# A two-block network on one Trainium2 core: the MLP's second projections in two phases, seven products for token tiles 0 and 2, residuals by halves of a tile's columns

## The reference

```python
def _sqrelu_mlp(h, w1, w2):
    return jnp.square(jax.nn.relu(h @ w1)) @ w2          # w1: 1024 x 4096, w2: 4096 x 1024
...
        x = _layer_norm(DN_ALPHA * x + (1.0 + g_t) * y, ln_g[i, 0], ln_b[i, 0])
        h = x * (1.0 + sc_c) + sh_c
        y = _sqrelu_mlp(h, mlp_w1[i], mlp_w2[i])
        x = _layer_norm(DN_ALPHA * x + (1.0 + g_c) * y, ln_g[i, 1], ln_b[i, 1])
```

## Time and profile before

| | us |
|---|---|
| median of three runs (3334.27, 3338.92, 3338.95) | 3338.92 |
| the profiled execution | 3333.77 |
| its span | 3331.80 |
| TensorE busy in it | 3149.7 |
| VectorE busy in it | 1541.2 |
| mean clock granted to TensorE, of full speed | 0.973 |
| layer 0: second projection, first to last product | 2356.9 to 2579.4 |
| layer 1: second projection, first to last product | 3098.5 to 3318.4 |

### The profile page before, as it was taken

The page is one execution under the profiler, slowest core; times in us unless marked ns, Lnnn a source line. Parts: engine busy times, 40 slices in busy tenths (PEclk is TensorE's granted clock), DMA queues, the critical chain, the costliest instruction groups (busy, mean ns, idle before and its releaser), DMA issues. The chain is left out here.

```text
span 3331.8 us, 37758 instructions
## 1 busy us (share of the span) xinstructions
PE 3149.7 (95%) x12154; PEld 1717.4 (52%) x12155; DVE 1541.2 (46%) x3359; ACT 563.3 (17%) x1281; POOL 243.0 (7%) x377
## 2 busy tenths in 40 slices
PE   7999999999998897979997988999999998999998
PEld 3445666644447332323333535488544565588543
DVE  6447676565556342334444386565103333565003
ACT  1002222200011121212222216200000233100000
POOL 1000000011100121212212000000000000000000
PEclk9999999999997998989999999999999999999999
DMA  7563133397733898997978311122221223022220
GB/s 242 167 205 96 61 98 89 102 308 241 243 127 128 327 353 336 365 358 302 349 283 288 112 56 39 51 95 76 84 104 27 79 74 133 26 95 101 76 76 25
DMA packets 261211, 532.85 MB, mean 160 GB/s; under 512 B 26249, under 2 KB 162052, under 8 KB 236522
## 3 DMA queue, kind: packets, MB, share of 16 engines
q1 hardware_dynamic: 204240, 380.16, 32.4%
q0 software_dynamic: 46992, 140.37, 12.2%
q10 hardware_dynamic: 9866, 10.82, 0.9%
HBM read 520.60 MB, written 36.83 MB: 167 GB/s over the span
## 5 line engine op out<-in xcount | busy, mean ns | idle before, releaser
L1328 PE MATMUL ps<-WR,hT 128*64 x832 | 384.8, 617 | 58.9 <-DVEq L2865 31.8
L1329 PE MATMUL ps<-WR,hT 128*64 128x512 f32 x832 | 384.8, 617 | 0.0
L1730 PE MATMUL ps<-WR 128*128 128x512 f32 x768 | 329.9, 592 | 0.0
L1328 PEld LDWEIGHTS ps<-WR,hT 128*64 128x64 f32 x832 | 117.3, 143 | 311.6 <-issue 311.6
L1730 PEld LDWEIGHTS ps<-WR 128*128 128x128 f32 x768 | 145.9, 190 | 182.8 <-issue 182.2
L2862 DVE COPY WR<-WR 128x1024 f32 x208 | 131.1, 693 | 227.1 <-SPq L646 174.0
L2625 DVE TENSOR_TENSOR WR<-ps,grow 128x1024 f32<-128x1024 f32 x20 | 24.5, 1224 | 436.3 <-PE ps L1741 368.5
L1024 PE MATMUL ps<-hT,WR 128*128 128x512 f32 x512 | 223.9, 593 | 0.6 <-DVE WR L2438 0.6
L1691 PE MATMUL ps<-WR 128*128 128x256 f32 x960 | 217.0, 379 | 0.0
L1691 PEld LDWEIGHTS ps<-WR 128*128 128x128 f32 x960 | 182.4, 190 | 24.8
L1349 PE MATMUL ps<-WR 128*64 x416 | 189.5, 598 | 3.2 <-DVEq L2875 2.1
(11 more groups left out here) (411 smaller groups left out, 4537.4 us busy)
## 6 DMA issues: line engine op xcount, KB each, us to landing
WR<-in_w_gate SPq DMA_DIRECT2D x64, 1024.0 KB, 8.7
WR<-in_w_up SPq DMA_DIRECT2D x64, 1024.0 KB, 11.3
WR<-in_w_down SPq DMA_DIRECT2D x64, 1024.0 KB, 9.1
WR<-in_mlp_w SPq DMA_DIRECT2D x32, 2048.0 KB, 7.7
xr<-in_ada_w POOLq DMA_DIRECT2D x32, 1024.0 KB, 5.6
WR<-in_w_in SPq DMA_DIRECT2D x56, 512.0 KB, 6.8
xr<-in_w_ada POOLq DMA_DIRECT2D x16, 1024.0 KB, 5.5
WR<-in_w_in SPq DMA_DIRECT2D x16, 1024.0 KB, 6.6
```

The costliest lines, as they stand in the source:

```text
L1328: mm(out[0:HALF], xT[u][:, k, 0:HALF], wa[:, :, k, :], start=(k == 0), stop=(k == KD - 1))
L1329: last = mm(out[HALF:P], xT[u][:, k, HALF:P], wb[:, :, k, :], start=(k == 0), stop=(k == KD - 1))
L1730: last = mm(ps[:, 2 * t + n, :], h1T[:, k, t * P:(t + 1) * P], w[:, k - 4 * u, 512 * n:512 * n + 512], start=(k == 0), stop=False)
```

## The change

The down stage becomes two phases. In phase 1 (`down_pair`, weights in the new stage `seven`) the outputs of token tiles 0 and 2 are made by seven products for each pair of k-tiles (k, k + 16): the blocks are the two k-tiles, the two token tiles and the two halves of 512 output columns. The row sums (`row_sums`, of h1T, 256 columns for two k at once) and the weight sums (`down_weight_sums`, 512 columns) are made by VectorE; each product has one bank and accumulates over the 16 pairs. At the end ScalarE copies p1 and VectorE adds the products into the corners `down_c` (`down_corners`, seven additions). In phase 2 the whole of w2 is loaded again, and token tiles 1 and 3 are made as before, tile 1 in banks 6 and 7, tile 3 in 4 and 5. The slots of the down stage's units are now 2, 1, 3, 2, 1, 3, 2, 1, those of `seven` are 1, 3, 2, 1, 3, 2, 1, 3; slot 0 holds sums and corners until the residual of tile 2 has read them.

The tiles of residuals 3 and 5 go in the order 0, 2, 1, 3. In layer 0 the transposes of tiles 0 and 2 stand behind units 1 and 2 of phase 2, those of tile 1 after the tenth product of tile 3, those of tile 3 at the end. `res_b` is raised once for each half of 512 columns, and every residual from banks (`by_halves`: n = 0, 2, 4 in all tiles, 3 and 5 in tiles 1 and 3) works on each half when it is there. The slots of the last weights of an output projection are given free by VectorE (`release`). In residual 5 normalizing, gain and store go by halves as well.

The diff, cut to its core. The stages `("seven0", 1, [(1, 2), (3, 2), (2, 2), (1, 2), (3, 2), (2, 2), (1, 2), (3, 2)])` and `seven1` stand ahead of the down stages.

```diff
+DOWN_BANKS = dict(p6=4, p5=0, p7=1, p4=2, p3=3, p1=6, p2=5)
+TILES_OF = {n: (0, 2, 1, 3) if n in (3, 5) else (0, 1, 2, 3) for n in range(6)}
+RES_B = {0: 0, 2: TT, 3: 2 * TT, 4: 2 * TT + 2, 5: 3 * TT + 2}
+TURN_BANK = {n: (0, 6, 2, 4) if n == 4 else (0, 2, 4, 6) for n in range(6)}
...
+        if i + 1 == UP_PAIRS:
+            v += ["t_0"] + [f"{n}_{i}" for n in CORNERS[:5]] + ["s_0"] + [f"{n}_{i}" for n in CORNERS[5:] + ("sq",)]
+        else:
+            v += [f"{n}_{i}" for n in CORNERS + ("sq",)]
+    p += [f"kp_{k}" for k in range(16)] + ["p1_end"]
+    a.append("p1_end")
+    v.append("t_1")
+    for j in range(1, 8):
+        v += [f"s_{j}", f"t_{2 * j}", f"t_{2 * j + 1}"]
+    v += [f"{n}_end" for n in CORNERS]
...
-    ("down0", 1, [(1, 1), (3, 1), (2, 1), (0, 1), (3, 1), (2, 1), (1, 1), (0, 1)]),
+    ("seven0", 1, [(1, 2), (3, 2), (2, 2), (1, 2), (3, 2), (2, 2), (1, 2), (3, 2)]),
+    ("down0", 1, [(2, 1), (1, 1), (3, 1), (2, 1), (1, 1), (3, 1), (2, 1), (1, 1)]),
...
+        down_t = [[view(WR, 512 * n, 512) for n in range(4)], [view(R, 16384 + 512 * n, 512) for n in range(4)]]
+        down_s = [[view(R, 18432 + 1024 * i + 256 * n, 2, P) for n in range(4)] for i in range(2)]
+        down_c = [view(WR, 2048 + D * i, D) for i in range(2)]
+
+        def weights_of(layer, k):
+
+            w = unit(f"seven{layer}", k // 2, 0, 4, D)
+            return [[w[:, 2 * i + k % 2, 512 * n:512 * n + 512] for n in range(2)] for i in range(2)]
...
+                    fill(f"seven{layer}", u, 0, *[(unit(f"seven{layer}", u, 2 * D * i, 2, D),
+                                                   mlp_w2[layer][:, 16 * i + 2 * u:16 * i + 2 * u + 2, :])
+                                                  for i in range(2)])
...
-            for t in range(TT):
-                sp.wait_ge(sem("res_x"), 5 * TT + t + 1)
-                sp.dma_start(out_v[:, t, :], xr[:, t, :]).then_inc(sem("out_done"), 16)
-            sp.wait_ge(sem("out_done"), 16 * TT)
+            for n, t in enumerate(TILES_OF[5]):
+                for h in range(2):
+                    sp.wait_ge(sem("res_x"), 5 * TT + 2 * n + h + 1)
+                    sp.dma_start(halves(out_v[:, t, :])[h], halves(xr[:, t, :])[h]).then_inc(sem("out_done"), 16)
+            sp.wait_ge(sem("out_done"), 2 * 16 * TT)
...
-                    if t == TT - 1 and n == KD - 1:
-                        spent(last, name, 0)
-                if hi == 2 * KD:
-                    last.then_inc(sem("res_b"), 1)
+                    if k == KD - 1:
+                        last.then_inc(sem("res_b"), 1)
...
+            def down_pair(layer, k):
+
+                name = f"seven{layer}"
+                (b11, b12), (b21, b22) = weights_of(layer, k)
+                s1, s2, s3, s4 = [v[:, k % 2, :] for v in down_s[(k // 2) % 2]]
+                t1, t2, t3, t4 = down_t[k % 2]
+                a11, a12, a22 = [h1T[:, i, t * P:(t + 1) * P] for i, t in ((k, 0), (k + 16, 0), (k + 16, 2))]
+
+                def product(p, rows, weights):
+                    if k == 0:
+                        pe.wait_ge(*bank_read(layer, DOWN_BANKS[p], 7 * (UP_PAIRS - 1)))
+                    return mm(ps[:, DOWN_BANKS[p], :], rows, weights, start=(k == 0), stop=(k == 15))
+
+                if k % 2 == 0:
+                    have(name, k // 2)
+                    pe.wait_ge(*up_v(layer, f"s_{k // 2}"))
+                pe.wait_ge(*up_v(layer, f"t_{k}"))
+                product("p6", s2, t2)
+                product("p5", s1, t1)
+                product("p7", s3, t3)
+                if k == 14:
+                    pe.wait_ge(*up_v(layer, f"sq_{UP_PAIRS - 1}"))
+                product("p4", a22, t4)
+                product("p3", s4, b22).then_inc(sem("up_p"), 1)
+                last = product("p1", a11, b11)
+                if k == 15:
+                    last.then_inc(sem("up_p"), 1)
+                last = product("p2", a12, b21)
+                if k % 2:
+                    spent(last, name, k // 2)
...
+                for k in range(16):
+                    down_pair(layer, k)
+                bank_free = {(1, 1): up_v(layer, f"c21_{UP_PAIRS - 1}"), (1, 0): up_a(layer, "p1_end"),
+                             (3, 0): up_v(layer, "u2_end"), (3, 1): up_v(layer, "c11_end")}
+                bank = {1: 6, 3: 4}
...
-                        pe.wait_ge(*up_v(layer, f"sq_{k // 2}" if k > 1 else f"sq{k}"))
-                        for t in range(TT):
-                            for n in range(2):
+                        for t in (1, 3):
+                            for n in ((1, 0) if t == 1 else (0, 1)):
                                 if k == 0:
-                                    pe.wait_ge(*bank_read(layer, 2 * t + n, 7 * (UP_PAIRS - 1)))
-                                last = mm(ps[:, 2 * t + n, :], h1T[:, k, t * P:(t + 1) * P],
+                                    pe.wait_ge(*bank_free[t, n])
+                                last = mm(ps[:, bank[t] + n, :], h1T[:, k, t * P:(t + 1) * P],
                                           w[:, k - 4 * u, 512 * n:512 * n + 512], start=(k == 0), stop=False)
                     spent(last, name, u)
+                    if layer == 0 and u in (1, 2):
+                        turn_in(2 * u - 2, xr, "res_norm", TT * 3, 4)
...
+                down_tile(1, 0, 16)
+                down_tile(3, 0, 10)
                 if layer == 0:
-                    last_turn(3, early)
+                    turn_in(1, xr, "res_norm", TT * 3, 4)
+                down_tile(3, 10, 16)
+                if layer == 0:
+                    turn_in(3, xr, "res_norm", TT * 3, 4)
...
+                for v in halves(xr[:, t, :], 2 if n == 5 else 1):
+                    A(v, v, ACT.Identity, scale=rstd[:, t:t + 1], bias=rtmp[:, 1, t:t + 1]).then_inc(
+                        sem("res_norm"), 1)
...
+                act.wait_ge(*up_p(layer, "p1_end"))
+                A(down_c[0][:, 0:512], ps[:, DOWN_BANKS["p1"], :], ACT.Copy).then_inc(sem("up_a"), 1)
...
+                def by_halves(n, t, alpha, scratch, at, done):
+
+                    for h in range(2):
+                        dve.wait_ge(sem("res_b"), done + h + 1)
+                        if t == TT - 1:
+                            release(n, h)
+                        x, g, v = [halves(w)[h] for w in (xr[:, t, :], grow[:, :], scratch)]
+                        link(V.tensor_tensor(v, ps[:, at + h, :], g, ALU.mult))
+                        link(V.scalar_tensor_tensor(x, x, alpha, v, ALU.mult, ALU.add))
+                        link.mark(V.bn_stats(stats[:, t, 6 * h:6 * h + 6], x))
+                    rms_of(t)
+                    shift_of(t)
+
+                def release(n, h):
+
+                    name, u = last_weights[n]
+                    if h == 1 or u == 1:
+                        dve.sem_inc(used[ring.slot(name, u if h else 0)], 1)
+
+                def shift_of(t):
+
+                    link(V.scalar_tensor_tensor(rtmp[:, 1, t:t + 1], mv[:, t, 0:1], -1.0, rstd[:, t:t + 1],
+                                                ALU.mult, ALU.mult))
+                    dve.sem_inc(sem("res_stats"), 1)
...
+                        at, tiles = 2 * t, TILES_OF[n]
+                        if n in (3, 5):
+                            at = {1: 6, 3: 4}.get(t)
+                            tiles = (1, 3)
+                        if t in tiles:
+                            done = 2 * (RES_B[n] + tiles.index(t))
+                            by_halves(n, t, alpha, scratch, at, done)
+                            return
+                        link(V.tensor_tensor(scratch, down_c[t // 2], grow[:, :], ALU.mult))
+                        if t == 2:
+                            dve.sem_inc(used[ring.slot(f"sums{n // 2 - 1}", 0)], 1)
...
-                    link(V.tensor_tensor(xr[:, t, :], xr[:, t, :], lngb[:, 0, :], ALU.mult))
-                    V.tensor_tensor(xr[:, t, :], xr[:, t, :], lngb[:, 1, :],
-                                    ALU.add).then_inc(sem("res_x"), 1)
+                    for h, (v, g, b) in enumerate(zip(*[halves(w, parts) for w in (xr[:, t, :], lngb[:, 0, :], lngb[:, 1, :])])):
+                        if h:
+                            dve.wait_ge(sem("res_norm"), done + 2)
+                        link(V.tensor_tensor(v, v, g, ALU.mult))
+                        V.tensor_tensor(v, v, b, ALU.add).then_inc(sem("res_x"), 1)
...
+            def row_sums(layer, j):
+
+                s1, s2, s3, s4 = down_s[j % 2]
+                a = lambda k, t: h1T[:, 16 * k + 2 * j:16 * k + 2 * j + 2, t * P:(t + 1) * P]
+                if j >= 2:
+                    dve.wait_ge(*up_p(layer, f"kp_{2 * j - 3}"))
+                link(V.tensor_tensor(s1, a(0, 2), a(1, 2), ALU.add))
+                link(V.tensor_tensor(s2, s1, a(0, 0), ALU.subtract))
+                link.mark(V.tensor_tensor(s3, a(0, 0), a(0, 2), ALU.subtract))
+                link(V.tensor_tensor(s4, a(1, 0), s2, ALU.subtract))
```

(102 more changed lines are left out.)

32 lines of the change are left out of this document (13 added, 19 removed), and 2 rows, old and new, of the table STAGES.

## The result

The changed kernel takes **3307.80 us** (median of 4 runs, 3299.74 to 3308.32), the kernel before on the same chip 3338.93 (4 runs, 3334.27 to 3343.27). That is 31.1 us less by the medians. The ratio, which goes by the means of the runs, is 0.9901, with a 95% interval of [0.9881, 0.9922]. The profiled execution took 3308.32 us, with a span of 3306.5 and a mean granted clock of 0.973, as before.

What follows compares the result with a forecast made beforehand. TensorE, busy for 95% of the span, was taken as the bound. The terms -27.5 + 1.0 - 1.0 - 1.5 - 2.8 = -31.8 us, set against the median of 3338.92, gave 3307.1 us, with a range of 3300 to 3317.

Steps and rivals of the forecast that it cites:

- Products: Second projections of both layers: 240 products for 256, 13.75 us less in each layer, 27.5 us in both.
- Sums: Phase 1: VectorE's row and weight sums take 7.6 us per two k against TensorE's 12.0, so cost nothing.
- Seam: Start of phase 1: the first product waits for the first row sums, TensorE losing 0.5 us a layer, +1.0 in all.
- Layer 0's transposes: Tiles 0, 2 and 1 ready before TensorE wants them; tile 2 tightest with 1.9 us of room; nothing, bound +3.
- Last tile of layer 0: Tile 3's residual by halves, with VectorE held by gained(1), shortens TensorE's stand of 7.91 us to 6.9: -1.0.
- Output projections: Behind each attention's output projection, halves remove TensorE's 0.77 us wait for the last tile's norm: twice 0.77, -1.5.
- First block: Residual behind w_o: halves cost about 0.35 us per tile and gain 1.4 on the first; nothing, between -0.5 and +1.5.
- The end: Behind the last product: last residual, normalizing and gain by halves -2.1, smaller last store -0.7; together -2.8 us.
- (A): Only the products count; hT's waiting, longer instruction chains and overheads eat what the halves give: near 3313; chance 0.15.
- (B): TensorE waits about 1.5 us more at each phase start and 3 at tile 2's layer 0 transposes: 3316; chance 0.13.
- (C): Slower: VectorE's sums pace phase 1; whole gain and 0.2% more lost from 14.4 us per two k; chance 0.03.
- (D): TensorE is not relieved by operands VectorE wrote or by 16 products fewer; time within 0.2%; chance 0.03.

## Why the prediction was right

3307.1 us was forecast and 3307.80 measured. The mechanism was the one forecast, and each rival has a measurement against it. The agreement to 0.7 us is partly luck: the second part fell by 34.0 us where 31.8 were forecast, and the part ahead of it moves by more than that difference from execution to execution. By the steps:

- **Products, -27.5.** Layer 1's second projection is 13.66 us shorter, and putting the eighth product back costs 26.3 in both layers (27.5 less 0.6 that the seams give back and 0.3 of the varying stretch make 26.6). Price and count were right.
- **Sums, hidden.** 7.7 us per two k for 7.6, and 53.3 us busy in phase 1. The expected sign "some 61" was eight times 7.6, gaps included, set against a figure that counts busy time alone.
- **Seam, +0.5 a layer.** 0.31. The four row sums took 1.68 us for the 1.8 counted, and the first product begins 0.16 behind them (3089.14 to 3089.30): 0.31 behind its old place. What was added on top of the bare difference was too much.
- **Weights and the change of phases, nothing.** The w2 loads are issued as two of 1 MB, which land 6.6 us after their issue, and even two slots were enough. No wait stands between phases.
- **Layer 0's transposes, nothing, with room of 1.9 us at tile 2.** Its normalization ends at 2499.98 + 1.24 = 2501.22 (ScalarE's timeline), and TensorE asks at 2503.20: 2.0 us of room.
- **Last tile of layer 0, -1.0.** 7.91 to 6.76: -1.15. VectorE was held by gained(1), as counted.
- **Output projections, -1.5.** Both waits are gone, and each was worth 1.0 us for the 0.77 of its bracket (8.02 us for 9.0, as above): -2.0. Reading the price off the bracket missed the 0.2 us that a wait adds around itself.
- **First block, nothing.** This step was wrong by 0.7 us, inside its bound. I had set the lead of the first tile (1.4) against the overheads (0.35 a tile). The trace shows why the lead is lost. ScalarE's and VectorE's timelines of the changed kernel, tile 1:

```profile
970.73 2.90 ACT L1861 ACTIVATE hT<-ps,mod 128x128 f32<-128x128 f32 x8 [13.06 <-PE ps L987]
973.48 1.27 ACT L2052 ACTIVATE xr<-xr,rtmp,rstd 128x1024 f32<-128x1024 f32 x1
...
974.79 1.22 DVE L2754 TENSOR_TENSOR xr<-xr,lngb 128x1024 f32<-128x1024 f32 x1 [3.22 <-ACT xr L2052]
```

  VectorE has the statistics of tile 1 ready at 971.57, 0.8 us earlier than before (972.39), although TensorE's transposes of tile 0 stand 0.84 us later in this execution (970.10 for 969.26): a lead of 1.6 us. But ScalarE takes its work in order, and tile 1's normalization lies behind the scaling of tile 0's transposes, which come when TensorE reaches them. VectorE gets there early and waits 3.22 us for 1.57 before. The lead is gone and the overheads stay. That the wait goes with whole tiles and stays with the halves alone is shown by three runs.
- **The end, -2.8.** 13.4 to 10.96 us (3295.54 to 3306.5): -2.45. From the last product to the last gain's end it is 8.53 us for 10.36, -1.8 for the expected -2.1. Of the missing 0.3, 0.2 is ScalarE's: two halves take 1.52 us where one whole takes 1.24, so that the first gain starts 0.84 us behind ScalarE's start (3301.32 - 3300.48) for 1.27 before, 0.4 won where I had counted 0.6. The store gives -0.6 for -0.7: 256 KB land in 2.0 us, 512 KB in 2.6. By the Trainium skill, "DMA: Bandwidth & Descriptors", Anatomy of one DMA, the estimate was 0.6, and the trace agrees with that difference. It does not agree with the two durations: by the page's constants, stated for GpSimd's path, they would be an estimated 2.6 and 3.2 us, and these stores of SyncE's took 0.6 less each.
- **Not foreseen.** In layer 0 the 32 records behind the stand took 15.69 us for 16.81: -1.1. They are matmuls of which a part runs at half rate: the granted clock is 0.89 over 15.9 us here and was 0.83 over 17.1 us before. The 52 records that begin the output projection of the second attention took 24.41 us for 24.93: -0.5. Both stretches vary with the execution (below).

By these, the second part should be -27.5 + 0.6 - 1.15 - 2.0 - 2.45 = -32.5, and with the two unforeseen pieces -34.1, for -34.0 measured. The forecast for it was -31.8.

**The rivals.** (A) lost because the halves keep 6.5 us of the second part. (B) lost since no wait of more than 0.3 us stands at a phase's start, and the room at tile 2 was as counted. Nor would small leaks have cost the clock here: with the weight sums made twice TensorE waited eight times, 1.0 to 1.4 us each, in phase 1, and the granted clock of the stage stayed 1.00. But it was busy for 98.1 of those 106.9 us. Short waits are not harmless everywhere. In the kernel before, at the end of the second attention, TensorE's timeline and the table by stage (columns as in the earlier trace rows) show this:

```profile
2816.91 0.33 PE L1550 MATMUL ps<-ident,WR 128*128 128x128 f32 x1 [1.77 <-DVE WR L3023]
2820.20 1.12 PE L1574 MATMUL ps<-ident,WR 128*128 128x128 f32 x4 [2.11 <-ACT WR L2169]
...
2811.00:2817.00 6.00, 3.53 (x29) 2.81 (x27) 2.24 (x14) 3.90 (x18) 0.00 (x0) 1.00 0.52 175
...
2820.00:2828.00 8.00, 4.64 (x13) 2.01 (x13) 5.42 (x18) 4.18 (x12) 0.00 (x0) 0.50 0.01 3
```

Behind waits of 1.77 and 2.11 us, with little work around them, the granted clock was 0.50 (1.2 GHz), as it was behind the stand of 7.91 us.

(C) was made to happen and cost 22.8 us, with its threshold at 12 us of sums per two k; the change stands at 7.7. (D) fell with the first record count. The same kernel gave a median of 3303.71 in another set of runs.

## What to carry to other kernels

Where TensorE is busy without a gap and VectorE has time to spare (26.5 us of 219.9 here), trade products for sums, and compute VectorE's work per period against TensorE's: below it costs nothing, above it costs the excess. Splitting work at the end of a chain pays where everything downstream can start on the half; where an engine in order stands between with other work in front, the lead is lost and only the overhead is left. If the whole execution varies by more than the effect, cut the span at a point ahead of the change and compare the parts.

## What the runs showed beyond what I expected

- **Executions differ ahead of the change, hardly behind it.** The second part starts anywhere from 2158.0 to 2169.2 us in ten profiled executions, while the second part of one kernel repeated to 0.1 us (1138.4 twice). What still moves the second part, by up to 1.9 us between runs whose phase 1 is alike, are the two stretches of the next point.
- **The stretches in which the clock comes back have no fixed price.** The 32 records behind layer 0's last transposes took between 15.42 and 16.95 us in ten executions, and the length of the stand in front does not order them (behind 7.9 us: 16.81 and 16.30; behind 6.8 us: from 15.42 to 16.95). The 52 records that begin the second attention's output projection took between 24.31 and 25.06.
- **A buffer that waits for its load need not matter.** 27.1 us of VectorE's waits for weights in 96.2 us cost TensorE nothing, since they took the place of waits for TensorE.
